# Spreading the context's output projection over x's attention in a two-block transformer kernel

## What is computed

```
h  = rms_norm(x,  norm_mix) * (1 + sc1)  + sh1
hc = rms_norm(xc, norm_mix) * (1 + sc1c) + sh1c
# x's queries see the keys of both streams, the context's only their own
a  = rms_norm(diff_attention(...), subln) * (1 - lam_init)   # 4 heads
nb = neighbourhood_attention(...)                            # 8 heads
y  = concat(a, nb) @ w_out          # x's output projection
yc = concat(ac, nc) @ w_out         # the context's
x  = x + g1 * y;    xc = xc + g1c * yc
h2 = rms_norm(x, norm_ffn) * (1 + sc2) + sh2                 # and hc2 from xc
x  = x + g2 * expert_choice_ffn(h2, router, w1, w3, w2)      # and xc from hc2
```

## Time and profile before

| | |
|---|---|
| median of 3 runs | 2757.0 us (2756.06 to 2761.44) |
| the profiled execution: its own time | 2762.46 us |
| its span | 2760.4 us |
| mean granted TensorE clock | 0.963 of full speed |
| busy over the span | PE 90%, DVE 35%, ACT 19%, POOL 2% |
| chain that ended last | PE 73%, DMA 20%, DVE 3%, issue 2% |
| HBM read | 695.30 MB |

### The profile page before, as it was taken

One profiled execution on the slowest core, in us unless ns is written; L12 is line 12 of the kernel. 1 busy time (PEld: TensorE's weight loads), 2 busy tenths in 40 slices (PEclk: granted clock), 3 DMA queues, 4 the chain that ended last, 5 costly groups with the idle time before them and its releaser, 6 DMA issues.

```text
span 2760.4 us, 26795 instructions
## 1 busy us (share of the span) xinstructions
PE 2493.9 (90%) x10589; PEld 1406.4 (51%) x10589; DVE 958.0 (35%) x1628; ACT 511.7 (19%) x906; POOL 49.3 (2%) x63
## 2 busy tenths in 40 slices
PE   8999999999999999999999899998889998665656
PEld 4546755464548764567776563433335764221212
DVE  6452454545551454542235542111114242000001
ACT  2102321012123311123123520000003141000001
POOL 0000000000000000010000100000000000000000
PEclk9999999999999999999999899999999999788878
DMA  7458754563468374665431259999998218999998
GB/s 277 153 200 274 242 214 152 198 244 107 177 228 280 113 254 152 225 172 144 136 100 63 76 209 406 421 422 422 422 422 296 102 66 340 421 421 422 422 422 339
DMA packets 237477, 700.93 MB, mean 254 GB/s; under 512 B 16888, under 2 KB 126632, under 8 KB 190184
## 3 DMA queue, kind: packets, MB, share of 16 engines
q1 hardware_dynamic: 230176, 686.73, 65.7%
q10 hardware_dynamic: 5088, 8.33, 0.9%
q0 software_dynamic: 2112, 4.46, 0.9%
HBM read 695.30 MB, written 4.06 MB: 253 GB/s over the span
## 4 chain that ended last, share of the span: by engine, by line
PE 73%; DMA 20%; DVE 3%; issue 2%; SPq 1%; ACT 1%; POOL 1%; ACTq 0%; DVEq 0%
PE bank L588 70%; DMA ring<-moe_w 19%; PE bank L597 2%; SPq L3577 1%; POOL AR L3531 1%; ACT AR L2923 1%; DMA AR<-hot 0%; DVE AR L1855 0%; DVE AR L2440 0%; DMA ring<-m_w_out 0%; ACT L2923 0%; DVE AR L1852 0%; DVE AR L1864 0%; DMA AR<-vec 0%; DVE H L1858 0%
## 5 line engine op out<-in xcount | busy, mean ns | idle before, releaser
L588 PE MATMUL bank<-ring,AR 128*32 128x512 f32 (+3 forms) x3656 | 897.5, 667 | 198.4 <-DMA ring<-moe_w 191.0
L588 PEld LDWEIGHTS bank<-ring,AR 128*32 128x32 f32 (+2 forms) x3656 | 329.6, 150 | 719.9 <-issue 688.2
L588 PE MATMUL bank<-H,ring 128*128 128x256 f32 (+3 forms) x2288 | 519.6, 389 | 3.2 <-issue 1.5
L2923 ACT ACTIVATE AR<-bank 128x512 f32<-128x512 f32 (+3 forms) x306 | 174.7, 576 | 1681.9 <-PE bank L588 1116.8
L588 PEld LDWEIGHTS bank<-H,ring 128*128 128x128 f32 (+2 forms) x2288 | 426.9, 189 | 89.8 <-issue 26.9
L588 PE MATMUL bank<-AR 128*128 128x512 f32 (+15 forms) x1456 | 407.7, 451 | 17.9 <-DVE AR L2784 6.2
L588 PE MATMUL bank<-ring,H 128*128 128x256 f32 (+3 forms) x1536 | 407.6, 501 | 0.7 <-DMA ring<-ada_w 0.7
L1852 DVE TENSOR_TENSOR AR<-AR,bank 128x512 f32<-128x512 f32 (+2 forms) x156 | 97.1, 624 | 762.0 <-PE bank L588 761.5
L588 PEld LDWEIGHTS bank<-ring,H 128*128 128x128 f32 (+1 forms) x1536 | 228.8, 170 | 153.3 <-issue 114.4
L588 PEld LDWEIGHTS bank<-AR 128*128 128x128 f32 (+7 forms) x1456 | 211.8, 186 | 166.0 <-issue 134.8
L1852 DVE TENSOR_TENSOR SX<-ring 128x1024 f32<-128x1024 f32 (+3 forms) x48 | 77.9, 1624 | 256.5 <-PE bank L588 256.5
(11 more groups left out here) (144 smaller groups left out, 911.8 us busy)
## 6 DMA issues: line engine op xcount, KB each, us to landing
ring<-moe_w SPq DMA_DIRECT2D x368, 1024.0 KB, 15.2
ring<-ffn_w SPq DMA_DIRECT2D x104, 1024.0 KB, 10.4
ring<-ada_w SPq DMA_DIRECT2D x48, 1024.0 KB, 5.4
ring<-m_w_in SPq DMA_DIRECT2D x26, 1024.0 KB, 12.0
ring<-ffn_w SPq DMA_DIRECT2D x32, 768.0 KB, 7.0
ring<-even_w_in SPq DMA_DIRECT2D x24, 1024.0 KB, 7.1
AR<-moe_w SPq DMA_DIRECT2D x18, 512.0 KB, 6.8
ring<-m_w_out SPq DMA_DIRECT2D x8, 1024.0 KB, 11.4
```

Source lines behind the costliest of these rows:

```text
L588: ins = pe.matmul(o, lhsT, rhs, start=start, stop=stop, skip_group_check=True)
L2923: return act.activation(o, i, func, **kw)
```

## The change

It moves work and neither adds nor removes any.

- PE: a half of the context's projection stands at every second value of `between`'s argument (0, 2, 4, ..., 14) where it stood at 0, 1, 3, 4, 6, 7, 9, 10. The head sums move from 12 and 14 to 16 and 18, the sum of squares from 16 to 20.
- DVE: the additions of the chunks move from 3, 6, 9, 12 to 4, 8, 12, 16; the scaling of the context from 19 and 20 to 22 and 23.
- ACT: squares from 4, 7, 10, 13 to 5, 9, 13, 17; head logarithms from 14 and 16 to 18 and 20; the root from 18 to 22; the shift from 21 to 24.
- Behind the attention the context's router stands behind the first two halves of x's projection, and the steps of its routing about one half later.
- SP: the router's weights are loaded behind x's first projection chunk.

```diff
-                    c, half = u // 3, u % 3
-                    if c < 4 and half < 2:
+                    c, half = u // 4, u % 4 // 2
+                    if c < 4 and u % 2 == 0:
...
-                    if u in (12, 14):
-                        head_sum("x", (u - 12) // 2, 7)
-                    if u == 16:
+                    if u in (16, 18):
+                        head_sum("x", (u - 16) // 2, 7)
+                    if u == 20:
                         late_sum("moe0_c", 7)
...
-                    router(0, 1, 7)
                     emptied(pe, "x.o11")
                     pe.wait_ge(sig("ye_x"), 2)
                     x_out(0, 0)
+                    x_out(0, 1)
+                    router(0, 1, 7)
+                    x_out(1, 0)
                     logit_turns(0, 1, 4)
-                    x_out(0, 1)
                     token_turns(0, 1, 0, (5, 6))
-                    x_out(1, 0)
+                    x_out(1, 1)
                     affinity_turns(0, 1, 4)
-                    x_out(1, 1)
+                    x_out(2, 0)
                     token_turns(0, 1, 1, (7, 5))
-                    x_out(2, 0)
                     x_out(2, 1)
+                    x_out(3, 0)
                     index_rows(0, 1, 6)
-                    x_out(3, 0)
                     x_out(3, 1)
...
-                    if u in (3, 6, 9, 12):
-                        c = u // 3 - 1
+                    if u in (4, 8, 12, 16):
+                        c = u // 4 - 1
...
-                    if u in (19, 20):
-                        ctx_scaled("moe0_c", 4 * (u - 19), 4 * (u - 18))
+                    if u in (22, 23):
+                        ctx_scaled("moe0_c", 4 * (u - 22), 4 * (u - 21))
...
-                    if u in (4, 7, 10, 13):
-                        c = u // 3 - 1
+                    if u in (5, 9, 13, 17):
+                        c = u // 4 - 1
                         emptied(act, f"even.c_out{c}")
...
-                    if u in (14, 16):
-                        head_log("x", (u - 14) // 2)
-                    if u == 18:
+                    if u in (18, 20):
+                        head_log("x", (u - 18) // 2)
+                    if u == 22:
                         root("moe0_c")
-                    if u == 21:
+                    if u == 24:
                         ctx_shift("moe0_c", 3)
...
                 output(T["even_w_out_2"])
+                columns_of(T["even_w_out_2"], 0)
                 router(0)
-                output(T["even_w_out_2"])
+                for c in range(1, 4):
+                    columns_of(T["even_w_out_2"], c * 256)
                 router(0)
```

## The result

| | kernel before | changed kernel |
|---|---|---|
| median, runs | 2758.2 us, 6 runs (2756.1 to 2763.7) | 2768.9 us, 6 runs (2764.8 to 2773.3) |
| ratio, 95% interval | | 1.0035 (1.0025 to 1.0044) |
| profiled execution, its span | 2762.46, 2760.4 us | 2773.28, 2771.2 us |
| six runs in a later comparison | 2759.1 us (30 runs) | 2768.1 us, ratio 1.0032 (1.0020 to 1.0044) |

The change makes the kernel slower by 9.7 us (the ratio on 2758), interval 6.9 to 12.1. I had forecast +5.7.

The account below looks back on a forecast made before the run. PE's path was taken to bound the kernel up to the expert layer, whose weight stream waits on it; 11.2 − 8.5 + 1.2 + 1.8 = +5.7 us on a median of 2757.0 gave 2762.7 us, range 2755 to 2768.

Parts of the forecast that it names:

- Term 1: x's attention: the sum of squares ends 11.2 us later, 8.5 of work ahead of it plus 2.7 of added waits.
- Term 2: End of x's attention: from DVE's first scaling to the last output's end takes 12.9 us instead of 21.45, 8.5 less.
- Term 3: Router, moved from an empty gap into PE's dense work at x's projection: +1.2 us, bounds 0.9 and 1.33.
- Term 4: Start of x's projection: the clock falls behind the emptied gap of 2.87 us, +1.8 us, bounds 0 and 3.7.
- It falls further: Rival: the clock loses more at x's projection, +1.9 and up to 3.7 more; 2764.6 to 2768 us, chance 0.23.
- The levels hold: Rival: the clock holds at the output behind turns 20, its sum and x's projection; 2759.1 us, chance 0.25.
- The fill works: Rival: PE finds inputs ready at every unit of x's attention, so term 1's waits disappear; 2751 us, chance 0.07.
- Nothing reaches the end: Rival: the stream of transfers in the expert layer swallows PE's delay; 2757 to 2758 us, chance 0.14.
- The routing becomes the limit: Rival: PE waits up to 3.55 us between logit_turns and affinity_turns for the softmax; 2766 us, chance 0.03.

Follow-up runs that it names:

- second profile: The changed kernel unaltered, run and profiled again in a later comparison: 2768.1 us, ratio 1.0032.
- third: Changed kernel plus six unread products in the 1.31 us wait ahead of turns 14 of the odd layer's attention: median 2764.8 us, ratio 1.0022.
- even fill: Kernel before plus 34 unread products in PE's waits in x's even attention and ahead of x_out(0, 0): 2757.6 us, ratio 0.9990.
- router only: Kernel before with only the context's router, its routing steps and its load moved as in the change: 2761.1 us, ratio 1.0013.
- scaling one later: Kernel before with DVE's context scaling at units 20 and 21 and ACT's shift at 22: 2760.0 us, ratio 1.0002.

## Why the prediction was right or wrong

The sign and the mechanism were right; the size was not. The median of 2768.9 lies 0.9 above my range, and I had given slower by over 0.2% only 0.42, less than the 0.51 for within 0.2%. The kernel before was 2758.2 in this comparison and not 2757.0; the ratio on 2757.0 gives 2766.6, inside the range. But +9.7 is far from +5.7 however one counts, and it is the width of the range that takes it in.

**Term 1, waits: right.** I had 6.7 us ahead of the sum of squares. They are 1.56 + 0.44 + 0.67 + 0.55 + 0.44 + 0.28 + 2.35 = 6.3. Turns 1 came at 1.56 (I had 1.75), around turns 16 at 0.72 (0.7), the output behind turns 20 at 2.35 (2.25).

**Term 1, total: 13.1 in the first profile against 11.2.** The sum ends 91.9 behind c_out0's start, before it was 78.8 (1553.93 − 1475.14). Of the missing 1.9, 1.8 is c_out2's half at the lower level (5.38 against 3.62). I had priced 0.5 us of wait at 0.5 us. In the second profile the half kept its level and the sum ended 11.1 later (1559.28 + 3.72 − 1473.13 = 89.9, less 78.8): term 1 as forecast.

**Term 2: right.** From the scaling's start to the output's end 13.2 us against 12.9, that is −8.2. The scaling starts 2.28 behind the sum (2.27 forecast), at 1568.56 behind 5.46 of idle time on DVE. I had given "near 1567.5". PE waits 5.73 ahead of turns 22 and 2.37 ahead of the output, where I had 5.6 and 2.4.

**Term 3: right.** The router adds 1.1 to 1.2 (1.17 with the level at 1.00 in both kernels).

**Term 4: 1.7 in the second profile and in two experiments (13.48 against 11.80), 2.5 in the first and third** (14.36 and 14.30), against 1.8. By the rule of the Trainium skill (TensorE: Matmul & The Clock Gate, section "HAM oscillation — how this bites in real kernels") I had weighed 3.7. The page's case has waits of some 3 to 5 us; here the wait was 2.81, the level did fall behind it in all five profiles with the gap empty and unfilled, and none shows a loss of 3.7.

**Sum on the path.** +6.0, +6.8 and +8.6 in three profiles of the changed order; +5.7 forecast. They differ by falls of the level, not by waits. Each is one profile against the one profile of before, whose levels differ between executions too.

**What failed** is the sentence "I count a shift of PE's path at the end of the attention one to one, up to the kernel's end". Two stretches that the change doesn't touch broke it, and I had put both at nothing. At the gather products 1.5 us of the shift went, since it was the kernel before that had lost its level there. From there to 2246 us it held (6.0 of 6.3). Then the clock fell behind a wait of 1.31 that stands in both kernels, 4.6 us in that profile. I had left those rows out, because the change doesn't touch that stretch. By the fill the odd wait is worth 2 to 3 us of the changed kernel's time. In the profile of before that I read, the level held there. With the +6.0 that the path shows in the second profile that makes 8 to 9, against the 9 to 10 measured. The fill of the same place in the kernel before (with the even fill, −3.6 instead of −2.2) gave 1.4, within the error of such a difference; so whether the changed kernel falls there more often, or earlier starts only make it so by chance, stays open. Of 12 profiles without that fill 6 fell: none of the three without a fill and with the norms where or nearly where they stood (before, router only, scaling one later), six of the nine others, too few to tell.

**The rivals.** "It falls further" came nearest (2764.6 to 2768, chance 0.23), with its loss in other places than x_out. "The levels hold" is not seen in any unfilled profile of the changed order. "The fill works" fell as argued: the waits stayed. "Nothing reaches the end" fell: the long run moved by 6.27. "The routing becomes the limit" fell: the gather products still wait 2.18 and 0.70 for DVE, as they did before (2.17 and 0.70).

## What to carry to other kernels

A wait on TensorE costs its own length and, behind it, perhaps the clock of what follows. So price every wait twice, and look for such waits in the whole kernel, for a level may fall in a stretch that the change doesn't touch. And a dependent chain (sum, logarithm, scaling, shift) moved late ends behind the last work that could hide it: from the scaling to the end of the attention it took 13 us, in which PE waited 1.06 and 2.37 and most of 5.73. Products whose result nobody reads kept the level in such waits and made the path shorter, not longer; 40 of them put into the kernel before gained 3.6 us, more than any order tried here.

## What was not expected of the hardware

- The level after the same waits differs between executions. Behind 0.67 and 0.55 us of wait one half took 5.38 in one profile and 3.69 in four; behind 1.31 us the odd attention's end was at the lower level in 6 of 12 profiles; behind 2.18 and 0.70 the gather products took 4.04, 5.56 or 6.4. The Trainium skill (TensorE: Matmul & The Clock Gate, Part 1, "The HAM clock gate", under "What's actually happening") says that the count of slow products at a kernel's start varies from run to run of one kernel. These profiles show the same in the middle of one.
- Short waits are enough: the lower level stood behind 0.55 (with 0.67 just before), 1.31, 1.84, 1.96 and 2.35. With the gap ahead of x_out(0, 0) empty (2.81) the projection began at the lower level in five profiles of five; with the router in it (1.11 to 1.54 idle) x_out(0, 0) took 3.69 in four of four unfilled ones. With the waits filled by products the clock was 1.00 over 45 us in all five such profiles.
- A fall costs 1.7 to 2.5 us at x's projection, 1.5 to 2.4 at the gather products (5.56 and 6.4 against 4.04) and 4.6 at the end of the odd attention.
